# Expert stage: a head's choice of experts cut into thirteen pieces, one behind each of thirteen dot products

## The reference

```python
q = (tok @ wq).reshape(n, PEER_HEADS, 2, PEER_HALF)
s = jnp.einsum('nhsd,hskd->nhsk', q, subkeys)
top_s, top_i = lax.top_k(s, PEER_TOPK)
cand = (top_s[:, :, 0, :, None] + top_s[:, :, 1, None, :]).reshape(n, PEER_HEADS, PEER_TOPK * PEER_TOPK)
best_s, best_j = lax.top_k(cand, PEER_TOPK)
i1 = jnp.take_along_axis(top_i[:, :, 0], best_j // PEER_TOPK, axis=-1)
i2 = jnp.take_along_axis(top_i[:, :, 1], best_j % PEER_TOPK, axis=-1)
expert = i1 * PEER_KEYS + i2
gate = jax.nn.softmax(best_s, axis=-1)
act = gelu(einsum('nd,nhkd->nhk', xb, take(u_tab, eb)))
out = einsum('nhk,nhkd->nd', gb * act, take(v_tab, eb))
```

## Time and profile before

| | |
|---|---|
| time, median of 3 runs | 4181.46 us (4180.76 to 4182.44) |
| span of the profiled execution | 4168.4 us |
| expert stage, from the first u gather to the end | about 2815 to 4168 us |
| PE busy, whole span | 90% |
| DVE busy | 49% |
| ACT busy | 17% |
| POOL busy | 19% |
| row gathers (queue q0) | 73728 packets, 536.90 MB |
| HBM read | 863.87 MB |

### The profile page before, as it was taken

The page is one execution under the profiler, slowest core; times in us unless marked ns, Lnnn a source line. Parts: engine busy times, 40 slices in busy tenths (PEclk is TensorE's granted clock), DMA queues, the critical chain, the costliest instruction groups (busy, mean ns, idle before and its releaser), DMA issues. The chain is left out here.

```text
span 4168.4 us, 80943 instructions
## 1 busy us (share of the span) xinstructions
PE 3753.8 (90%) x35591; PEld 2292.0 (55%) x35591; DVE 2050.6 (49%) x3418; ACT 717.9 (17%) x1304; POOL 783.5 (19%) x755
## 2 busy tenths in 40 slices
PE   7999999999999989999999999989977777777776
PEld 3466666666666655666668888656422223222222
DVE  1355565555555546777772000036454554554544
ACT  2223222322223212122121000010110100100101
POOL 3000000001000000001000000004544444444532
PEclk9999999999999999999999999999999999999998
DMA  9211111111111116665564444429999999999997
GB/s 382 92 36 49 47 49 38 44 42 47 50 37 49 36 30 229 189 210 161 183 192 159 155 162 163 188 84 419 402 405 427 404 408 427 406 407 427 406 427 309
DMA packets 394620, 872.98 MB, mean 209 GB/s; under 512 B 16684, under 2 KB 234430, under 8 KB 325054
## 3 DMA queue, kind: packets, MB, share of 16 engines
q0 software_dynamic: 73728, 536.90, 30.8%
q1 hardware_dynamic: 228864, 284.82, 19.9%
q10 hardware_dynamic: 91710, 46.43, 3.9%
HBM read 863.87 MB, written 4.23 MB: 208 GB/s over the span
## 5 line engine op out<-in xcount | busy, mean ns | idle before, releaser
L2571 PE MATMUL ps<-w_slots,diag 128*128 128x512 f32 x1920 | 899.9, 615 | 286.5 <-DMA w_slots<-in_peer_v,ixv 252.4
L2571 PEld LDWEIGHTS ps<-w_slots,diag 128*128 128x128 f32 x1920 | 356.9, 195 | 827.5 <-issue 507.4
L979 PE MATMUL ps<-hT,w_slots 128*128 128x512 f32 (+1 forms) x1536 | 630.5, 538 | 3.1 <-PEq L230 2.2
L1719 PE MATMUL ps<-hT,w_slots 128*128 128x256 f32 (+1 forms) x1504 | 500.1, 486 | 6.5 <-PEq L655 4.9
L2348 DVE SCALAR_TENSOR_TENSOR junk<-w_slots,hT 128x2048 f32<-128x2048 f32 x128 | 293.4, 2292 | 291.6 <-DMA w_slots<-in_peer_u,ixu 288.5
L2348 DVE SCALAR_TENSOR_TENSOR junk<-ybT,hT 128x2048 f32<-128x2048 f32 x128 | 293.4, 2292 | 273.6 <-DMA ybT<-in_peer_u,ixu 271.8
L2238 POOL DMA_INDIRECT w_slots<-in_peer_v,ixv x244 | 291.4, 1194 | 499.7 <-PE ps L2571 465.1
L1719 PEld LDWEIGHTS ps<-hT,w_slots 128*128 128x128 f32 x1504 | 281.6, 190 | 173.3 <-issue 152.7
L979 PEld LDWEIGHTS ps<-hT,w_slots 128*128 128x128 f32 x1536 | 267.5, 190 | 177.6 <-issue 153.9
L2441 ACT ACTIVATE diag<-ident,coef 128x128 f32<-128x128 f32 x240 | 94.6, 400 | 934.7 <-PE ps L2571 924.9
L695 POOL TENSOR_TENSOR bonus<-Kh 128x256 f32<-128x256 f32 x16 | 11.8, 735 | 1175.4 <-DVE Kh L916 1175.4
(11 more groups left out here) (393 smaller groups left out, 4752.7 us busy)
## 6 DMA issues: line engine op xcount, KB each, us to landing
w_slots<-in_w_mod SPq DMA_DIRECT2D x128, 512.0 KB, 4.8
w_slots<-in_w_in SPq DMA_DIRECT2D x56, 1024.0 KB, 5.6
w_slots<-in_w_in ACTq DMA_DIRECT2D x44, 1024.0 KB, 6.7
w_mod_ring<-in_w_mod SPq DMA_DIRECT2D x16, 2048.0 KB, 13.6
w_slots<-in_w_in SPq DMA_DIRECT2D x7, 4096.0 KB, 13.7
w_slots<-in_w_branch_a SPq DMA_DIRECT2D x4, 4096.0 KB, 13.4
w_slots<-in_w_branch_b SPq DMA_DIRECT2D x4, 4096.0 KB, 13.6
w_slots<-in_w_out SPq DMA_DIRECT2D x4, 4096.0 KB, 12.8
```

The lines of the kernel that those rows point to most:

```text
L979: last = mm(ps[:, 4, t0:TOK], w[m % 2][:, k, :], hT[:, k, t0:TOK], start=(k == 0), stop=(k == KC - 1))
L1719: last = mm(out, w[m % SLOTS_W][:, k, :], hT[:, k, t0:TOK], start=(k == 0), stop=(k == KC - 1))
L2571: last = nc.tensor.matmul(ps[:, 4 * n + c, :], diag[:, k % 2, :], vb[k % NB][:, c * 512:(c + 1) * 512], start=False, stop=False)
```

## The change

`choose(i)` is cut into functions and takes a second argument k: without it, all pieces run as before; with it, only piece k. `emit_u` calls `choose(chosen, k)` behind dot product k, for k = 0 to 12, and no longer the whole ahead of dot product 4. The difference for the softmax (`diff`) moves from behind `idx` to ahead of `pf`. `MID` goes from 8 to 13, in all turns: `ixu` and `ixv` are copied ahead of dot product 13. On ACT the exponent moves from ahead of `diag` 10 to ahead of `diag` 13. No instruction is added or taken away.

```diff
-            + ["hi", "lo", "pf", "eq0", "mul0", "red0", "eq1", "mul1", "red1", "ef", "idx", "diff", "sum", "rec", "gates"]), True)
+            + ["hi", "lo", "diff", "pf", "eq0", "mul0", "red0", "eq1", "mul1", "red1", "ef", "idx", "sum", "rec", "gates"]), True)
...
-        MID = TOPK // 2
+        MID = TOPK - 3
...
+                def halves(i):
                     dve.wait_ge(*DV.by("j21", i))
-
                     nc.vector.tensor_scalar(part_i[:, 0, :, :], best_j[:, :, :], 4, None, ALU.logical_shift_right).then_inc(*DV.did("hi"))
                     nc.vector.tensor_scalar(part_i[:, 1, :, :], best_j[:, :, :], TOPK - 1, None, ALU.bitwise_and).then_inc(*DV.did("lo"))
+                    nc.vector.tensor_tensor(soft[:, :, :], best_s[:, :, :], best_s[:, :, 0:1].broadcast_to([P, 2, TOPK]),
+                                            ALU.subtract).then_inc(*DV.did("diff"))
                     dve.wait_ge(*DV.by("lo", i))
                     nc.vector.tensor_copy(part_f[:, :, :, :], part_i[:, :, :, :]).then_inc(*DV.did("pf"))
...
-                    nc.vector.tensor_tensor(soft[:, :, :], best_s[:, :, :], best_s[:, :, 0:1].broadcast_to([P, 2, TOPK]),
-                                            ALU.subtract).then_inc(*DV.did("diff"))
                     wait_alone(dve, passed, *DV.by("idx", i))
+
+                def choose(i, k=None):
+
+                    if k in (None, 0):
+                        first_max(i)
+                    if k in (None, 1):
+                        first_places(i)
+                    if k in (None, 2):
+                        first_out(i)
+                    if k in (None, 3):
+                        second_max(i)
+                    if k in (None, 4):
+                        second_places(i)
+                    if k in (None, 5):
+                        sums_of_lists(i)
+                    if k in (None, 6):
+                        best_places(i)
+                    if k in (None, 7):
+                        best_out(i)
+                    if k in (None, 8):
+                        next_max(i)
+                    if k in (None, 9):
+                        next_places(i)
+                        halves(i)
+                    if k in (None, 10):
+                        hits(i, 0)
+                        hit_places(i, 0)
+                    if k in (None, 11):
+                        hits(i, 1)
+                        hit_places(i, 1)
+                    if k in (None, 12):
+                        rows_of_tables(i)
...
-                        if k == 4 and chosen is not None:
-                            choose(chosen)
                         if k == MID:
...
                         dot(u, n, k)
+                        if chosen is not None:
+                            choose(chosen, k)
...
-                        if chosen is not None and k == 10:
+                        if chosen is not None and k == 13:
                             exponent(chosen)
```

More of the change, by code:

```diff
@@ L2268, in _, with first_max @@
             def _(dve):
-                def choose(i):
+                flat = lambda m, n: m[:, n, :, :].rearrange("p a b -> p (a b)")
+                def first_max(i):
                     fresh(DV)
@@ L2276, in choose, with first_places @@
                         nc.vector.max(top_s[:, n, s, 0:8], sc[:, n, s, :]).then_inc(*DV.did(f"m1{n}{s}"))
+                def first_places(i):
                     for n, s in LISTS:
@@ L2279, in choose, with first_out, second_max @@
                         nc.vector.max_index(top_i[:, n, s, 0:8], top_s[:, n, s, 0:8], sc[:, n, s, :]).then_inc(*DV.did(f"i1{n}{s}"))
+                def first_out(i):
                     for n, s in LISTS:
                         nc.vector.match_replace(sc2[:, n, s, :], top_s[:, n, s, 0:8], sc[:, n, s, :], -3.0e38).then_inc(*DV.did(f"mr{n}{s}"))
+                def second_max(i):
                     for n, s in LISTS:
@@ L2284, in choose, with second_places @@
                         nc.vector.max(top_s[:, n, s, 8:16], sc2[:, n, s, :]).then_inc(*DV.did(f"m2{n}{s}"))
+                def second_places(i):
                     for n, s in LISTS:
@@ L2287, in choose, with sums_of_lists @@
                         nc.vector.max_index(top_i[:, n, s, 8:16], top_s[:, n, s, 8:16], sc2[:, n, s, :]).then_inc(*DV.did(f"i2{n}{s}"))
+                def sums_of_lists(i):
                     dve.wait_ge(*DV.by("i211", i))
@@ L2292, in choose, with best_places @@
                     wait_alone(dve, passed, *DV.by("cand", i))
-                    flat = lambda m, n: m[:, n, :, :].rearrange("p a b -> p (a b)")
                     for n in range(2):
                         nc.vector.max(best_s[:, n, 0:8], flat(cand, n)).then_inc(*DV.did(f"b1{n}"))
+                def best_places(i):
                     for n in range(2):
@@ L2298, in choose, with best_out, next_max @@
                         nc.vector.max_index(best_j[:, n, 0:8], best_s[:, n, 0:8], flat(cand, n)).then_inc(*DV.did(f"j1{n}"))
+                def best_out(i):
                     for n in range(2):
                         nc.vector.match_replace(flat(cand2, n), best_s[:, n, 0:8], flat(cand, n), -3.0e38).then_inc(*DV.did(f"br{n}"))
+                def next_max(i):
                     for n in range(2):
@@ L2303, in choose, with next_places @@
                         nc.vector.max(best_s[:, n, 8:16], flat(cand2, n)).then_inc(*DV.did(f"b2{n}"))
+                def next_places(i):
                     for n in range(2):
@@ L2310, in choose @@
                     nc.vector.tensor_scalar(part_i[:, 1, :, :], best_j[:, :, :], TOPK - 1, None, ALU.bitwise_and).then_inc(*DV.did("lo"))
+                    nc.vector.tensor_tensor(soft[:, :, :], best_s[:, :, :], best_s[:, :, 0:1].broadcast_to([P, 2, TOPK]),
+                                            ALU.subtract).then_inc(*DV.did("diff"))
                     dve.wait_ge(*DV.by("lo", i))
                     nc.vector.tensor_copy(part_f[:, :, :, :], part_i[:, :, :, :]).then_inc(*DV.did("pf"))
-                    dve.wait_ge(*DV.by("pf", i))
@@ L2314, in choose, with hits @@
[L2314 to L2324, removed]
+                def hits(i, s):
+                    dve.wait_ge(*DV.by("red0" if s else "pf", i))
+                    nc.vector.tensor_tensor(hot[:, :, :, :], part_f[:, s, :, :].unsqueeze(3).broadcast_to([P, 2, TOPK, TOPK]),
+                                            iota_f[:, :].unsqueeze(1).unsqueeze(1).broadcast_to([P, 2, TOPK, TOPK]),
+                                            ALU.is_equal).then_inc(*DV.did(f"eq{s}"))
@@ new lines, in hit_places, with rows_of_tables @@
+                def hit_places(i, s):
+                    dve.wait_ge(*DV.by(f"eq{s}", i))
+                    nc.vector.tensor_tensor(hot[:, :, :, :], hot[:, :, :, :],
+                                            top_f[:, :, s, :].unsqueeze(2).broadcast_to([P, 2, TOPK, TOPK]), ALU.mult).then_inc(*DV.did(f"mul{s}"))
+                    dve.wait_ge(*DV.by(f"mul{s}", i))
+                    nc.vector.tensor_reduce(ex[:, s, :, :], hot[:, :, :, :], AX, ALU.add).then_inc(*DV.did(f"red{s}"))
+                def rows_of_tables(i):
```

## The result

The changed kernel took 4144.03 us (median of four runs, 4141.39 to 4148.94) against 4181.11 us for the kernel before (median of four): ratio 0.9911, 95% interval 0.9897 to 0.9924. Over all sets of runs of this study the changed kernel has a median of 4144.8 us (14 runs, 4136.6 to 4154.3) and the kernel before one of 4178.4 us (55 runs, 4168.6 to 4187.6): 33.7 us apart, or 0.8%.

A forecast was written before the change was run, and what follows sets the result against it. The prediction took the expert stage's gathers, at 427 GB/s, as the bound. It summed 31.5 us in the loop and 1.0 in `first_v` to 32.5 us off 4181.46, giving 4149.0 us, range 4145 to 4158 us.

The forecast's parts named there:

- What bounds the kernel: Expert stage: bound by its gathers, 427 GB/s at DMA share 1.01, 78.50 us in a turn without a choice.
- The cost of the choice: Loop's twelve turns: 31.5 us lost, 5.3 for each of six choices, as POOL's pause runs the DMA engines dry.
- The pieces: Behind thirteen dot products: each piece fits DVE's idle 2.6 us, 0.4 us left in the worst two; 31.5 us gained.
- POOL behind the pieces: Chosen turns: a u gather's issue meets a piece, sits out 2.18 us at most with 1.6 us to spare; cost 0.
- `MID`: All turns: later row numbers delay POOL's first v gather 0.8 us, 1.1 to 1.6 in chosen turns; cost 0, turn 0 at most 2.8.
- The margin: Later row numbers at a turn's start: only a delay over ten us would cost, as the queue holds 15.0 us.
- `first_v`: Stage with the first choice: 1.0 us gained, between 0 and 1.9, since PE's order may keep what DVE gives back.
- the sum's base: Whole time: 32.5 us taken from the median 4181.46, with the span's 13.1 us below it held unchanged, giving 4149.0 us.
- half of the stall: Rival, chosen turns: late issues keep the queue shallow, so half the gain, 16 us, 4165 us; chance 0.10.
- POOL was not shut out: Rival, chosen turns: pieces hold POOL's issues, one gather in 4.9 us and not two, +30, 4211 us; chance 0.04.
- no other cause drained the queue: Rival, loop: the choice was not what drained the queue, so time stays at 4181 within 0.2%; chance 0.05.

The follow-up runs named there:

- long_block: Changed kernel with pieces 0 to 9 in one block behind dot product 3, pieces 10, 11, 12 behind dot products 5, 7, 9; 4142.01 us.
- longer_choice: Kernel before with two sums over 2048 elements (results unused) added to the choice's block; 4211.01 us.
- block_spaced: Changed kernel with the choice in one block behind dot product 3 and a sum over 2048 elements behind each of dot products 4 to 7; 4171.83 us.
- mid15: Changed kernel with both copies of row numbers ahead of dot product 15 instead of 13, in all turns; 4175.29 us.

## Why the prediction was right or wrong

**What bounds the kernel** held: the turns at 78.50 us are the gathers' own pace. None of the kernels got a turn of the loop much below it, and once POOL was in time only the first two turns of a loop came out longer (up to 79.5 us).

**The cost of the choice** held in kind and nearly in size. The loop was expected at 942.0 us and took 942.5, 941.8 and 942.8. What it takes off is 32.1 us against the mean of the two profiles of before (974.5), 31.5 against the one that was used: the chosen turns of that kernel differ by some tenths from execution to execution. long_block and longer_choice confirm that it is POOL's wait beyond a threshold, not DVE's time, that had cost.

**The pieces** fit as forecast, 0.54 us left in the worst case. **POOL behind the pieces**: the u gather's issue was stretched to 1.03 us and not to 2.2, and cost nothing. The rows tell the two kinds of instruction apart: an issue under the product (two inputs) ends 0.8 us behind it, and one under the sum of block_spaced (one input), at 3097.26 us, takes 0.94. (The one at 3098.50 starts 0.06 us ahead of a dot product and takes 0.94 too: a dot product does not hold an issue that started ahead of it.) By the rule of the Trainium skill, "SBUF — State Buffer", section "Who interferes with whom" (two SBUF inputs contend with GpSimd's reads, one doesn't), these rows agree.

**`MID`** cost nothing in the loop, as forecast, though POOL's wait grew by 2.3 us and not by 1.1 to 1.6 in a chosen turn, and by 1.5 us (2.57 to 4.03) and not by 0.8 in the others; the copy's landing in `ixv` and POOL's start are 1.0 us apart, which had been left out. In turn 0 the first v gather went 3.6 us later and not 2.8. The turn took 63.0 us in the mean against 62.0, where 0 was taken, but kernels with the same turn 0 took 61.5 to 63.3, so that 1.0 us is not shown to be a cost. The margin was overrated: the text spoke of a delay over ten us before it would cost. The copies are at a wait of 4.9 us, ahead of dot product 14 they were at 8.9 us for nothing and ahead of 15 at 13.8 us for 2.6 us a turn, so the margin is between 4 and 9 us. The queue was read in the same way, as 15.0 us or 12.5 us of reserve: by 12.5 a wait of 13.3 us would cost 0.8 us, and it cost 5.3.

**`first_v`** gained 1.6 us (94.2 to 92.6), where 1.0 was taken between 0 and 1.9. (Rows 11 cut it at 97.5 us, from an earlier start; the table cuts it from dot product to dot product.) As turn 0 became 1.0 us longer, and the border between the two moves, only their sum is firm: 156.3 to 155.6 us. Turn 1 stayed the same.

The terms add up to 32.1 + 1.6 - 1.0 = 32.7 us for the 32.5 forecast; the expert stage as a whole lost 1350.2 - 1317.1 = 33.1.

**The step that failed is the sum's base**, the 4181.46 us from which the gain was taken, and the range, which gave that base no room. "The span is 13.1 us under the median of the runs; with that unchanged, 4181.46 - 32.5." Those 13.1 us were not what lies around a span, which is 1.7 to 1.8 us in every later run. They said that the profiled execution was a quick one, and single executions of this kernel turned out to be spread over 19 us. The median of three, 4181.46, stood 3.0 us above the pooled 4178.4. The miss of 4.9 us (4148.96 to 4144.03) is made up of these 3.0, of 1.2 us by which the gain was taken too small (33.7 over all runs against 32.5), and of 0.7 us by which the first set of the changed kernel lies under its pooled median of 4144.8. With the right base and the forecast's own gain the time is 4145.9, inside the range. The range covered only what the edit might do, with 4 us below the forecast, and nothing for a base and a result that are medians of three and four runs, where single runs have a standard deviation of 4.1 us (before) and 4.9 us (after). So it was partly luck on which side of 4145 the result fell: the two later sets of the changed kernel have medians of 4141.8 and 4145.5 us, one outside the range and one inside. The mechanism was right. The rivals were all worse: half of the stall stayed in none of the chosen turns, POOL was not shut out, and in the loop no other cause drained the queue. Outside the loop one did, PE at the start of turn 1, in both kernels.

## What to carry to other kernels

Where a stage is bound by gathers through a few buffers, work on the engine that frees the buffers costs nothing as long as the engine that issues is never held for longer than its queue lasts, here more than 8.9 us and by an estimate about 11; it needn't be cut to the size of the gaps, and two blocks did what thirteen pieces did. Look for the loss in the issuing engine's longest wait, and read its length against the time from issue to landing. And compare the time less the span before using it as a constant: where it is far from what other profiles of such kernels show (here 1.8 us), the profile is of another execution than the median's, and the range has to hold the spread of single runs.

## What the runs showed of the hardware that was not expected

A queue of gathers that land 15.0 us after their issue covers a pause of only some 11 us (8.9 us cost nothing, 13.8 us cost 2.6). The traces account for most of the 4 us. The 15.0 us run from the start of an issue, which itself takes 0.94 us or more, and the bytes end about 13.8 us behind its end (14.8 us for a gather of u); the next gather's first bytes come only 1.65 us behind the start of its issue; and the rate is low at first (181 GB/s over 1.4 us in mid15). In mid15 the engines are quite empty for 0.6 us only, and the rest of its 2.6 us goes with low rates before and behind that; how it divides stays open. And dot products run back to back behind a pause make it dearer by 1.5 us or more, since each holds an issue that starts under it until 0.8 us behind its own end, and the bytes come as much later.
